# A two-layer decoder trunk: the fourth head pair's output transposes on three steps, and weight fetches between a pair's query and key copies

## What is computed

```
for l in range(2):
    h = LN(alpha*h + 0.5*SwiGLU_a(h))
    h = LN(alpha*h + Mixer(h))
    h = LN(alpha*h + 0.5*SwiGLU_b(h))
Mixer(h): p = h @ w_in, then side by side
    6 forgetting-attention heads (64 wide, causal, a cumulative log forget gate as bias)
    4 differential-attention heads (two softmaxes, p0 - lam*p1, ALiBi, RMS norm)
    6 chunked spatial gating heads
    y = concat(...) @ w_out
```

## Time and profile before

| | |
|---|---|
| median of 3 runs | 1940.44 us (1937.7 to 1941.63) |
| the profiled execution | 1940.12 us, its span 1938.4 us |
| PE busy | 1880.6 us, 97% of the span |
| DVE, ACT, POOL busy | 73%, 37%, 17% |
| mean granted TensorE clock | 0.990 |

### The profile page before, as it was taken

How to read it: one execution, slowest core, us unless ns; L and a number is a source line. 1 busy time by engine, 2 the same in 40 slices (tenths; PEclk the granted TensorE clock), 3 DMA queues, 4 the chain that set the end, 5 groups by cost and what they waited for, 6 DMA issues and landing times.

```text
span 1938.4 us, 24919 instructions
## 1 busy us (share of the span) xinstructions
PE 1880.6 (97%) x9113; PEld 1579.4 (81%) x9113; DVE 1407.4 (73%) x1997; ACT 709.8 (37%) x1070; POOL 335.8 (17%) x291
## 2 busy tenths in 40 slices
PE   7999999999999999999999999999999999999996
PEld 6888888889878888888888888888888888888884
DVE  6778777952566787787887777886446586778778
ACT  4232423334554324233233242333355442423321
POOL 5200000153314500000160000003343251000002
PEclk8999999999999999999999999999998999999998
DMA  5232223235732222222322222232557222222231
GB/s 221 74 116 92 108 87 130 95 118 179 210 96 88 104 92 108 87 108 87 131 87 109 87 108 87 108 114 101 175 159 202 71 93 87 108 87 108 87 130 43
DMA packets 41927, 217.07 MB, mean 112 GB/s; under 512 B 8724, under 2 KB 9172, under 8 KB 17928
## 3 DMA queue, kind: packets, MB, share of 16 engines
q1 hardware_dynamic: 38984, 200.35, 29.0%
q0 software_dynamic: 2880, 15.90, 3.5%
HBM read 198.28 MB, written 17.93 MB: 112 GB/s over the span
## 4 chain that ended last, share of the span: by engine, by line
PE 86%; DVE 6%; issue 2%; DMA 2%; ACT 2%; SPq 1%; POOL 1%; ACTq 0%; DVEq 0%; POOLq 0%
PE psum L949 79%; PE psum L1146 3%; DMA rawA<-in_a_w 2%; SPq L428 1%; DVE res L1410 1%; PE psum L1240 1%; PE psum L977 1%; DVE st L1434 1%; DVE negm L1742 1%; PE psum L1230 1%; DVE hl L1487 0%; ACT psum L873 0%; DVE xlo L1389 0%; PE psum L1340 0%; PE psum L1218 0%
## 5 line engine op out<-in xcount | busy, mean ns | idle before, releaser
L949 PE MATMUL psum<-xhi,whiA 128*128 128x512 f32 (+1 forms) x768 | 288.2, 375 | 10.3 <-DVE xlo L1389 10.3
L949 PE MATMUL psum<-whiD,hl 128*128 128x512 f32 x832 | 283.9, 391 | 3.6 <-DVE hl L1487 2.8
L949 PE MATMUL psum<-xlo,whiA 128*128 128x512 f32 (+1 forms) x768 | 286.6, 373 | 0.0
L949 PE MATMUL psum<-xhi,wloA 128*128 128x512 f32 (+1 forms) x768 | 286.5, 373 | 0.0
L949 PE MATMUL psum<-xhi,whiB 128*128 128x512 f32 x704 | 273.9, 389 | 0.0
L949 PE MATMUL psum<-xlo,whiB 128*128 128x512 f32 x704 | 273.9, 389 | 0.0
L949 PE MATMUL psum<-xhi,wloB 128*128 128x512 f32 x704 | 273.9, 389 | 0.0
L759 ACT ACTIVATE s<-psum 128x512 f32<-128x512 f32 x36 | 21.5, 598 | 576.3 <-PE psum L949 576.3
L1508 DVE SCALAR_TENSOR_TENSOR nat<-psum,nat 128x1024 f32<-128x1024 f32 x144 | 175.9, 1222 | 26.3 <-PE psum L949 26.3
L949 PEld LDWEIGHTS psum<-whiD,hl 128*128 128x128 f32 x832 | 156.2, 188 | 39.5 <-DVE hl L1487 4.5
L1508 DVE SCALAR_TENSOR_TENSOR res<-psum,res 128x1024 f32<-128x1024 f32 x108 | 132.0, 1222 | 76.1 <-PE psum L949 76.1
(11 more groups left out here) (205 smaller groups left out, 3586.7 us busy)
## 6 DMA issues: line engine op xcount, KB each, us to landing
rawA<-in_a_w SPq DMA_DIRECT2D x63, 1024.0 KB, 6.3
rawB<-in_b_w SPq DMA_DIRECT2D x54, 1024.0 KB, 4.7
rawD<-in_d_w SPq DMA_DIRECT2D x46, 1024.0 KB, 4.8
stacks<-hl SPq DMA_DIRECT2D x192, 64.0 KB, 1.8
whiD<-stacks POOLq DMA_DIRECT2D x10, 768.0 KB, 6.1
wloD<-stacks POOLq DMA_DIRECT2D x10, 768.0 KB, 5.7
gbr<-in_gb_row SPq DMA_DIRECT2D x7, 1024.0 KB, 8.3
stacks<-wloD SPq DMA_DIRECT2D x48, 64.0 KB, 1.7
```

The source lines that it names most:

```text
L949: ins = t_.matmul(out_, a_, b_, start=(start and k == 1), stop=(stop and k == n), skip_group_check=check)
```

## The change

Four things move; no instruction is added or removed. On SP, a pair's fill of slot A stands between `put_query` and `put_key`. On PE, the four output transposes go from two in each of steps 24 and 25 to one, two and one in steps 24, 25 and 26, and the first output product from the first to the second place of step 26; the lag of one piece is made up at output (4, 0), which shares its place with (4, 1). On ACT and DVE the copies follow (`EARLY_TURNS`), with ACT's high half of the output weights (`key_half` of slot 5) behind the copies of step 25. DVE's additions come one step later.

```diff
+EARLY_TURNS = [0, 1, 1, 2]
...
                 for b in range(1, BODIES):
                     put_query(b)
+                    fill("A", l * A_ALL + A_QK + b + 2)
                     put_key(b)
-                    fill("A", l * A_ALL + A_QK + b + 2)
...
                     exp(G)
+                    if b == EARLY_BODY and k == 0:
+                        y_hi(0)
                     if G:
                         p_out(G - 1)
                     if k == 0 and b + 1 < BODIES:
                         key(b + 1)
-                        key_half(b + 2)
+                        if b < EARLY_BODY:
+                            key_half(b + 2)
...
-                    if b == EARLY_BODY and k < 2:
-                        y_hi(2 * k)
-                        y_hi(2 * k + 1)
+                    if b == EARLY_BODY and k == 1:
+                        y_hi(1)
+                        y_hi(2)
+                        key_half(b + 2)
+                    if b == EARLY_BODY and k == 2:
+                        y_hi(3)
...
+                elif n == 0:
+                    pe.wait_ge(yt_ok, l * NC + 3 + u)
...
                 pe.wait_ge(qk_ok, (l + 1) * BODIES * 2 - 1)
-                for i in range(len(EARLY)):
-                    if i == 1:
-                        pe.wait_ge(qk_ok, (l + 1) * BODIES * 2)
-                    turn_y(l, i)
-                    yield
-                pe.wait_ge(yt_ok, l * NC + len(EARLY))
+                turn_y(l, 0)
+                yield
+                yield
+                pe.wait_ge(qk_ok, (l + 1) * BODIES * 2)
+                turn_y(l, 1)
+                turn_y(l, 2)
+                yield
+                yield
+                turn_y(l, 3)
+                yield
                 pe.wait_ge(lo_ok["B"], l * B_ALL + B_WO + 1 + AHEAD)
                 for u in range(8):
                     for n in range(len(EARLY) if u < WHOLE else 2):
+                        if u == 0:
+                            pe.wait_ge(yt_ok, l * NC + n + 1)
                         if n == 2:
                             pe.wait_ge(lo_ok["A"], l * A_ALL + A_WO + 1 + AHEAD)
                         early_output(l, u, n)
-                        yield
+                        if (u, n) != (4, 0):
+                            yield
...
-                    adds = G - EARLY_BODY * STEPS - NT
+                    adds = G - EARLY_BODY * STEPS - NT - 1
...
-                    if b == EARLY_BODY and k < 2:
-                        y_lo(2 * k)
-                        y_lo(2 * k + 1)
+                    for i in range(len(EARLY)):
+                        if b == EARLY_BODY and k == EARLY_TURNS[i]:
+                            y_lo(i)
```

## The result

The changed kernel takes 1955.37 us (median of 6 runs, 1950.32 to 3816.54), the kernel before 1940.51 in the same session. The ratio is 1.0074, 95% interval 1.006 to 1.0089: slower by 0.74%, 14.4 us by the ratio. The prediction was 1937.8 us in 1932 to 1944, so it was wrong in sign and its range missed by 11 us. One of the six executions was a disturbed one of 3816.54 us with a granted clock of 1.00, for a reason that nothing here shows, and as it was the profiled one, the profile after is that of the same kernel run again (the first experiment), 1956.35 us with a span of 1954.6.

The account below looks back on a forecast made before the run. TensorE, busy 97% of the span, was taken as the bound, leaving its idle time and clock. Layer 0 about 0 and layer 1 2.2, rounded to 2.3 us, off 1940.1 gave 1937.8 us; range 1932 to 1944.

Parts of the forecast that it names:

- The aim of the fetch: Projection weights for ACT: fill goes at 474.48, not 478.57; ACT's stall and TensorE's 1.24 and 0.68 us in layer 0 go.
- Sum of the fetch ... about zero: SP's moved fill, gains at ACT against new stack waits: -0.15 us in layer 0, +0.1 us in layer 1.
- Body 1 of layer 0: First scores of body 1: load goes at 483.65, lands at 489.55, TensorE waits 1.0 us, so body 0 wins 0.25.
- Layer 1: The fetch's part in layer 1: 0.4 us won from ACT waits less 0.3 at the last stack.
- For body 2's stack I take nothing: First scores of body 2: no loss counted for the later stack load.
- 0.6 lost at each: Bounds on the stack shifts if a landing differs by 0.6 us: all of 1.24 + 0.68 won, or this lost.
- The clock: Steps 24 to 28: shorter idle pieces leave the clock full or low no longer than layer 0; layer 1 wins 1.86 us.
- the signs that I named for a slower result: In the changed profile: clock at 0.50 for over ten us in either layer, or TensorE waiting over 1.5 us at body 4.
- The transposes: Steps 24 to 28: 0.9 us won less 0.7 for one output product paid back at (4, 0), net 0.2 in layer 0.
- the last pair's stack is late: Rival, chance 0.10: last keys' copies hang on ACT, POOL and SP; low half 3 us later costs 3 us twice, 1943.8.
- the clock stays low longer: Rival, chance 0.12: spread idle pieces hold 1.2 GHz from step 24 through body 3, up to 5 us a layer, 1945.8.
- the waits really go: Rival, chance 0.32: stacks land earlier, clock stays full, no new 0.7 us wait in step 28; 1933.7 us.

Follow-up runs that it names:

- the first experiment: The changed kernel itself run once more, unaltered, for a profile of an undisturbed execution: 1955.45 us, 1.007 to the kernel before.
- e2: Kernel before with only SP's fill of slot A moved between a pair's query and key copies, transposes as before: 1953.75 us, 1.0076.
- e3: Changed kernel with SP's order of before (fill behind the key copies), so the transposes' part alone: 1937.89 us, 0.9983 to the kernel before.
- e4: Changed kernel, but for the last pair SP copies the keys ahead of the fill, as before: 1948.73 us, 1.0049 to the kernel before.
- e7: Kernel before with the four fills of slot A issued by POOL right behind its low half, not by SP: 1944.11 us, 1.0023.
- e9: Kernel before with each slot A fill split in two of 512 KB, query weights' half ahead of the key copies, keys' half behind: 1939.29 us, 1.0006.
- e12: e9 with a further unused 512 KB DRAM-to-DRAM copy ahead of the key copies, without a wait: 1939.91 us, 1.0009 to the kernel before.

## Why the prediction was wrong

**The aim of the fetch: right.** Fill at 474.45 (forecast 474.48), ACT's stall at L694 gone, TensorE's ACT waits in layer 0 from 2.9 to 0.8 us (forecast 1.0). The weight's landing, 474.48 + 5.21, is 479.7 and not the 479.8 of the forecast; nothing hangs on it.

**"Sum of the fetch ... about zero": this step failed.** It was worth +11 us of span (e2). Its chain was right, two of its links were too short (when the load goes, and how long it takes to land), and it was followed in too few places:

- *Body 1 of layer 0*, forecast wait 1.0 us, measured 2.36. The copies began at 474.85 (forecast 474.95) and TensorE came at 488.39 (forecast 488.55). But the load went at 484.02, not 483.65, and its 768 KB took 6.2 us to land, not the 5.4 of the one row I priced it by the earlier trace rows. *Body 3*: forecast 0.7, measured 2.62, again by a load 0.5 us later than its place behind the body before and a landing of 6.4 us. Here the kernel before had the longer landing already: its own load for body 3 took 6.1 us, and I priced it by body 1's 5.4.
- *Layer 1*, where I counted only gains at ACT and 0.3 us at the last stack. Bodies 1, 2 and 3 each wait about 2 us, 6.2 in all. I had read no load, landing or arrival there. By layer 0's own numbers the load is due 483.65 - 469.29 = 14.36 us into the body (measured in e2: 14.36) and lands 5.9 us later, 20.3 us in. Body 0 of layer 1 took 1439.96 - 1420.63 = 19.33 us before, without the stall that body 0 of layer 0 has to give back. That is 0.9 us lost even at the short landing, and it could have been read from the first scores. With the 6.7 us that this load took before, it is 2.2 us; e2 waits 1.94.
- *"For body 2's stack I take nothing"* was right for layer 0 in e2, where no wait shows, and wrong for layer 1.

What I called the bounds, "0.6 lost at each", held neither for the landing (0.8 and 1.0 us longer) nor for the number of places: five in e2 and six in the changed kernel, of which I had priced two, and the last pair's.

**The clock: right for the transposes, and not asked for the new waits.** I weighed whether the idle pieces of body 3 hold the clock down, and in e3 they don't. But I had a 1.9 us wait behind which the clock falls, and priced new stack waits in us of idleness only, because I made them 1.0 us at most. Measured at 2.36 and 2.62 us, they are followed by a lower clock: in e2 it is 0.83 between 490 and 500 us and 0.66 between 540 and 550, though the second window also has the keys' wait of 1.9 us in it.

```profile
490.00:500.00 10.00, 9.25 (x51) 8.39 (x52) 5.18 (x17) 4.93 (x15) 2.37 (x1) 0.83 0.51 118
540.00:550.00 10.00, 6.93 (x41) 6.32 (x39) 5.96 (x17) 6.04 (x16) 2.37 (x1) 0.66 0.37 101
```

Of the signs that I named for a slower result, two came: over ten us at 1.2 GHz in either layer, and a wait of over 1.5 us at body 4 (2.03, in layer 1).

As to its price, 1.86 us for 6.6 us of low clock is 0.28 of the length, and 7.9 us for the 28 us of the changed kernel is 0.28 as well. The Trainium skill's "TensorE: Matmul & The Clock Gate" (Part 1) prices a low stretch at half its length. For 28 us that would be 14 us, an estimate by the page, and doesn't agree with the 7.9 us here. That is an account of one execution with a clock given to a hundredth (about 1.5 us of low clock for each stage and kernel), not a separate measurement.

**The transposes: right in place, and in size partly by luck.** 2.3 us forecast, 2.7 measured in e3. The steps came out so (e3's body 3 begins 0.31 us later than that of before): second transpose behind the keys at 539.69 after 1.48 us (forecast 1.3); row maximum of step 25 at 540.15 (540.0), of step 26 at 544.12 (544.0), of step 27 at 547.68 (547.7); the wait for `y_lo` 1.24 (1.2); TensorE's wait for ACT in step 28 0.66 (0.7).

```profile
539.69 1.25 PE L1177 MATMUL psum<-ident,nat 128*128 128x128 f32 x8 [1.48 <-DVE hl L1671]
...
543.66 0.66 PE L1177 MATMUL psum<-ident,nat 128*128 128x128 f32 x4 [1.24 <-DVE xlo L1720]
...
550.27 0.88 PE L1257 MATMUL psum<-vals,s 128*128 128x64 f32 x6 [0.66 <-ACT s L882]
```

From the first scores to the second head of body 4, layer 0 is 0.14 us shorter and layer 1 1.8, nearly the 0.2 and 2.1 of the forecast, but by larger parts that cancel. Body 3 wins 1.96 us in layer 0 and 3.82 in layer 1, since I had kept 3.4 us at the low clock in each and none is left; body 4 gives back 1.2 us in each layer (forecast: the 0.7 of one output product), body 0 of layer 0 1.16, and body 2 of layer 1 1.12. The last two lie in bodies whose code e3 doesn't change and are ACT's longer stalls at a projection weight, told with e3; one execution can't say whether they belong to the transposes.

**The rival "the last pair's stack is late"**, given 0.10, is a part of the loss in the changed kernel: e4 puts it at 6.7 us by medians. Its own point was nearly met in layer 0 (load at 562.20, 21.65 us into the body; forecast 555.8 - 535.4 = 20.4), and no wait shows there. In layer 1 the load goes 24.83 us into the body and TensorE stands 2.03 us. The low clock behind the stack wait of body 3 is not enough to explain this: it lies behind both, and from layer 0 to layer 1 the fill comes 1.52 us later into the body (14.41 for 12.89), but TensorE's arrival at body 4 does too, by 1.5 us. What is left is that SP takes 7.02 us for the twelve copies, and not 5.72, that the load follows 0.4 us later, and that it lands in 6.0 us and not 5.7. Why was not looked into.

**The rival "the clock stays low longer"**, given 0.12, was right that the clock would be low for much longer, but looked for the cause in the transposes, and e3 shows none there. Its 8 us at the full length is also not the sum of its parts, which give up to 5 us in each layer.

**The rival "the waits really go"**, given 0.32, fell at its first condition, no stack landed earlier than reckoned; and the wait of 0.7 us in step 28, which it left out, did come.

**The range** doesn't fit its own chances. I gave 0.19 to times above 1944.3 and yet ended it at 1944, as if only a tenth lay beyond. And no rival had stack waits of 2 us at bodies 1 to 3.

## What to carry to other kernels

When a transfer is moved ahead of others in one queue, its wait is put ahead of them too, and here it was the wait that cost: work out the new start of everything behind it, follow each to its last consumer, and do so at every place where the queue repeats, in every layer, from that place's own load and arrival. A margin between a landing and its consumer that shows no wait now can be nearly used up; read both times. Price a landing by the same load's own rows and by the slowest of its kind, not by one row of another body, and count the clock as one that may fall behind each new wait of about 2 us at TensorE. A fetch that must go early was cheaper here from a queue with nothing urgent behind it (e7, 1.0023), or in a part that is free by then (e9, 1.0006), than ahead of urgent small copies (e2, 1.0076), though none of the three was faster than the kernel before.

## What the runs showed of the hardware that I had not expected

- One kind of transfer lands in very different times. The four 768 KB loads for the first heads of bodies 1 to 4 took 5.4, 9.5, 6.1 and 5.5 us in layer 0 of the kernel before and 6.7, 9.6, 5.9 and 5.4 in layer 1, and the first of them 5.8, 6.2 and 7.2 us in e4, e2 and the changed kernel, whose SP orders are the same up to there. The first five of the keys' 64 KB strips took 1.7 us before and 4.6 behind a fill of 1 MB. The last strips took about as long as before (3.2 and 3.1), so the long landing of the first ones passed the lateness on only in small part: from the first copy to the load it is 9.17 us in e2, 8.70 before.
- The length of a single wait doesn't say whether the clock falls. The clock fell behind 1.90 us in the kernel before and stayed at 1.00 behind 2.03 us at body 4 of the changed kernel (window 1530 to 1540). In e3 TensorE stood 2.40 us at 486.75 and the clock stayed at 1.00 through the next ten us; in e2 it stood 2.36 us until 490.75 and the clock came down to 0.50. What differs between the two wasn't separated. The row and the window of e3, then two windows of e2:

```profile
486.75 0.43 PE L1257 MATMUL psum<-vals,s 128*128 128x64 f32 x2 [2.40 <-ACT s L882]
```

```profile
490.00:500.00 10.00, 10.00 (x64) 8.91 (x64) 6.09 (x21) 6.17 (x20) 2.59 (x2) 1.00 0.58 141
```

```profile
492.00:494.00 2.00, 2.00 (x13) 1.90 (x12) 0.98 (x4) 0.76 (x4) 0.00 (x0) 0.68 0.73 139
494.00:496.00 2.00, 2.00 (x8) 1.71 (x8) 1.29 (x3) 1.86 (x4) 0.29 (x1) 0.50 0.00 0
```

- More idleness at TensorE can come with less time: in e3 it is busy for 0.3 and 1.2 us less in the two windows of body 3 than before, and the body is 2.0 and 3.8 us shorter, at 2.4 GHz throughout. Before, the second window had 34 matmuls in 9.28 us of busy time at 1.2 GHz, and in e3 it has 54 in 8.08.
- Half a megabyte more within DRAM ahead of the copies cost 0.6 us by medians (e12 against e9), within what can be told from nothing, in a stage where the DMA engines are busy for half the time.
